# Value pass of an expert layer: one 512-column matmul with both parts of the gated activations in place of two of 256 columns

## The chip, the cores and the metric

The kernel runs on one core of a Trainium2 chip. The metric is the device time of one execution in microseconds (us); the median over several runs counts. The core has five engines that run beside each other and wait for each other on semaphores: TensorE (matmuls, PE in the profile, its weight loads are PEld), VectorE (DVE), ScalarE (ACT), GpSimd (POOL) and SyncE (SP), which issues most of the transfers. Matmul results go to PSUM, which has 8 banks of 512 float32 columns on each of 128 partitions.

## The reference, cut to what matters

Two layers of a decoder trunk over 256 tokens of width 1024. Each has a mixer and then a PEER channel mixer with 128 x 128 = 16384 single-neuron experts. The change lies in the second:

```
def peer(h, w_q, subkeys, u_tab, v_tab):
    ...                                  # top 16 experts for each of 8 heads
    act = gelu(einsum('td,thkd->thk', xc, u_tab[ec]))
    return einsum('thk,thkd->td', gc * act, v_tab[ec])
x = x + peer(h, ...)
```

The kernel gathers nothing. It computes all 16384 activations densely, multiplies them by gates that are zero where an expert was not chosen, and multiplies the result by the whole value table (16384 x 1024).

## The kernel before

**Precision.** The large products are done in a reduced float32 format (fp32r) in which a matmul is one record of the trace; plain fp32 matmuls leave two records each. To keep accuracy each operand is split in a high part (rounded) and a low part (the rest), and three products are summed: high weights by high data, high weights by low data, low weights by high data.

**The stream.** All weights come as tiles of 128 x 1024, 600 in order: `w_in`, `w_out`, `q0`, `u0`, `v0`, `qkv`, `w_o`, `q1`, `u1`, `v1`; `u` and `v` have 128 tiles each. SyncE loads a tile into one of four `raw` buffers as soon as it is free (L346). A tile is handled in halves of 512 columns: ScalarE rounds the high part into `w_hi` (L406), VectorE subtracts to get `w_lo` (L603). There are four half slots, so two tiles are ready or in work at a time. TensorE adds to the semaphore `half_used` at the end of each half, and ScalarE refills on it.

**The value pass** (`combine`, L1168 to L1184, once for each layer, 128 tiles). Tile i of `v` holds the values of 128 experts; their gated activations for 256 tokens are row i of the table `big`. ScalarE rounds a row into `ag_hi` (L537, the first two rows L542), VectorE makes `ag_lo` (L967), both double-buffered and two tiles ahead. TensorE runs over 8 blocks of 128 output channels, m = 0 to 7, and for each over the three products, with 256 token columns: L1180 (`w_hi` by `ag_hi`), L1181 (`w_hi` by `ag_lo`), L1182 (`w_lo` by `ag_hi`). Each matmul has its own load of weights. All three sum into `y_ps[:, m, :]`, 256 columns of PSUM; the eight accumulators lie in banks 0 to 3, two to a bank, and stay there through all 128 tiles. Banks 4 and 5 (`proj_ps`) are for projections, 6 and 7 (`misc_ps`) for the scatter of gates and for sums of squares; they are unused in the value pass.

**Behind the pass.** VectorE waits for the last half, and adds the eight accumulators to the residual `xT` (L980, 8 adds, semaphore `y_added`). ScalarE squares each block of `xT` as it comes (`square`, L436), and TensorE sums the squares with a matrix of ones (`sum_squares`, L1047, plain fp32, 8 matmuls, 16 records, into bank 6). The RMSNorm follows (VectorE L618 to L623, ScalarE L440), then the next projection (`qkv` in layer 0) or the output (layer 1). In layer 0 two tiles of `qkv` are still rounded and split before the adds. GpSimd waits for `y_added` in layer 0 to load the bias rows (L382).

**Before the pass** come the projections of the `u` tiles (L1035 to L1037, the same three products with 256 columns) with the scatter (L1147, plain fp32 matmuls of 60 or 68 columns). The first matmul of the value pass waits for `ag_ready`, which comes only when all gates are applied (`act_gated`, `late_gated`).

Of the kernel before, what the change touches and what calls it, by code (L numbers as in the profile page):

```python
# [21 lines left out]
F32R = mybir.dt.float32r  # L22
I32 = mybir.dt.int32
U32 = mybir.dt.uint32
ALU = mybir.AluOpType
# [3 lines left out]
P = 128  # L29
T = 256  # L30
TT = T // P
D = 1024
KD = D // P
# [41 lines left out]

GROUPS = T // 4


def bucket_of_distance():

    exact, span = REL_BUCKETS // 2, 2048
    out = []
    for n in range(T):
        if n < exact:
            out.append(n)
        else:
            f = np.float32(np.log(np.float32(n) / np.float32(exact))) / np.float32(math.log(span / exact))
            out.append(min(exact + int(np.float32(f * np.float32(REL_BUCKETS - exact))), REL_BUCKETS - 1))
    return out
# [41 lines left out]
def build(nc, a, out):  # L131
    ctx = ExitStack()
    with ctx:
        def sb(name, shape, dt=F32):
            return ctx.enter_context(nc.sbuf_tensor(name, shape, dt))

        def sem(name):
            return ctx.enter_context(nc.semaphore(name))
# [3 lines left out]
        xT = sb("xT", [P, KD, T])  # L142
# [6 lines left out]
        hot_j = sb("hot_j", [P, 8, P])  # L149
        hot_i = sb("hot_i", [P, 8, P])  # L150
        fresh = sb("fresh", [P, 2, T])
        ag_hi = sb("ag_hi", [P, 2, T], F32R)
        ag_lo = sb("ag_lo", [P, 2, T], F32R)
        const = sb("const", [P, 4 * P])
        gains = sb("gains", [P, 5, KD])
        small = sb("small", [P, 6, KC])
# [1 line left out]
        ident, anti, ones, iota = (const[:, P * i:P * (i + 1)] for i in range(4))  # L158

        psum = ctx.enter_context(nc.psum_tensor("psum", [P, 8, 512], F32))  # L160
        y_ps = psum[:, 0:4, :].rearrange("p b (m t) -> p (b m) t", t=T)
        proj_ps = [psum[:, 4 + i, 0:T] for i in range(2)]
        misc_ps = [psum[:, 6 + i, :] for i in range(2)]

# [14 lines left out]
        sq, _ = room(top - 2 * KD * T, KD, T)  # L179
# [69 lines left out]
        sq_ready = [sem(f"sq_ready{i}") for i in range(5)]  # L249
# [42 lines left out]
        hot_step = sem("hot_step")  # L292
        ag_hi_ready = sem("ag_hi_ready")
        ag_ready = sem("ag_ready")
        y_added = sem("y_added")
        staged = sem("staged")
        values_staged = sem("values_staged")
# [101 lines left out]
        def _(act):  # L399
# [29 lines left out]
                        ahead(name, k, j)  # L429
                sweep(act, turns, body)  # L430

            def square(r, sem_, count):

                for m in range(KD):
                    act.wait_ge(sem_, count(m))
                    act.activation(sq[:, m, :], xT[:, m, :], ACT.Square).then_inc(sq_ready[r], 1)  # L436

            def root(r):
                act.wait_ge(rstd_step[r], 2)
                act.activation(rstd[:], ms[:, 1, :], ACT.Sqrt).then_inc(rstd_ready[r], 1)  # L440
# [118 lines left out]
            ids_f_tmp = room(top - 2 * KD * T, UNITS, TOPK)[0]  # L559
            experts(0)  # L560

            square(2, y_added, lambda m: m + 1)
            root(2)
            split_operand(3)
            taking("qkv", lambda k, j: act.activation(z1[:, bass.ds(4 * k + j, 1), :].rearrange("p a t -> p (a t)"), proj_ps[j % 2],
# [23 lines left out]
            split_operand(4)  # L589
            only_ahead("w_o", 2)  # L590
            experts(1)
            square(4, y_added, lambda m: KD + m + 1)
            root(4)


# [1 line left out]
        def _(dve):  # L597
# [287 lines left out]
            def experts(l):  # L885
# [90 lines left out]
                        ahead(v, k, j)  # L976
                sweep(dve, NKEYS // 4, v_body, last=1)
                dve.wait_ge(half_used, 2 * (TILE0[v] + NKEYS))
                for m in range(KD):
                    dve.tensor_tensor(xT[:, m, :], xT[:, m, :], y_ps[:, m, :], ALU.add).then_inc(y_added, 1)  # L980
                dve.wait_ge(y_added, KD * (l + 1))

            add_residual("w_out")
# [37 lines left out]
        def _(pe):  # L1021
# [19 lines left out]
                sweep(pe, tiles // 4, lambda k: [project(name, k, j, operand) for j in range(4)],  # L1041
                      first=0 if operand is None else 1)

            def sum_squares(r):
                for m in range(KD):
                    pe.wait_ge(sq_ready[r], m + 1)
                    mm = pe.matmul(misc_ps[0][:, 0:T], ones, sq[:, m, :], start=(m == 0), stop=(m == KD - 1))  # L1047
                mm.then_inc(ss_ready[r], 1)


# [3 lines left out]
                      start=True, stop=True).then_inc(line_ps, 1)  # L1054
# [13 lines left out]
            for t in range(TT):  # L1068
                for c in range(KC):
                    mm = pe.transpose(psum[:, 2 + t, c * P:(c + 1) * P], vn[:, c, t * P:(t + 1) * P], ident)  # L1070
# [4 lines left out]
            for c in range(KC):  # L1075
                for t in range(TT):
                    for e in range(2):
# [3 lines left out]
                        mm = pe.matmul(o, ones[0:1, 0:HD], sgu_b[0:1, h, :], start=False, stop=True)  # L1081
# [32 lines left out]
            def experts(l):  # L1114
                q, u, v = f"q{l}", f"u{l}", f"v{l}"
                sum_squares(1 + 2 * l)
                pe.wait_ge(subk_in, 16 * (l + 1))

                def q_body(k):
                    for j in range(4):  # L1120
                        project(q, k, j, 2 + 3 * l)
                        if not (isinstance(k, int) and 4 * k + j == 0):
                            score_keys(l, k, j - 1) if j else score_keys(l, k - 1, 3)
                sweep(pe, 4, q_body, first=1)
                score_keys(l, 3, 3)
                projections(u, 4 * PICK_TURNS)
                pe.wait_ge(build_step, 23 * l + 15 + 7)
                for a_, src in enumerate((id_f[:, 0], id_f[:, 1], tv)):
                    for t in range(TT):
                        at = (a_ * TT + t) * P  # L1130
                        mm = pe.transpose(psum[:, at // 512, at % 512:at % 512 + P],
                                          src.rearrange("p (t u) r -> p t (u r)", t=TT)[:, t, :], ident)
                mm.then_inc(picks_ps, 1)

                def scatter(late, g, half):

                    rows = NKEYS - LATE if late else LATE
                    r = 2 * GROUPS * l + (0 if late else GROUPS) + g
                    if late:
                        at_least(pe, gates_stored, GROUPS * l + g - 1)  # L1140
                    elif isinstance(g, int) and g < 2:
                        pe.wait_ge(gates_stored, GROUPS * (l + 1))
                    else:
                        pe.wait_ge(act_gated, GROUPS * l + g - 1)
                    pe.wait_ge(hot_ready, r + 1)
                    for i in range(4):
                        mm = pe.matmul(misc_ps[half][:, i * rows:(i + 1) * rows], hot_j[:, 4 * half + i, :],  # L1147
                                       hot_i[:, 4 * half + i, 0:rows], start=True, stop=True)
                    mm.then_inc(scattered, 1)

                def late_body(k):
                    for j in range(4):
                        project(u, k, j)
                        for half in range(2):
                            scatter(True, 8 * (k - PICK_TURNS) + 2 * j + half, half)

                def early_body(k):
                    for j in range(4):
                        project(u, k, j)
                        if not (isinstance(k, int) and k == LATE_TURN and j == 0):  # L1160
                            scatter(False, 4 * (k - LATE_TURN) + j - 1, (j - 1) % 2)

                sweep_from(pe, PICK_TURNS, LATE_TURN, late_body, first=1)
                sweep_from(pe, LATE_TURN, NKEYS // 4, early_body, first=1)
                for g in range(NKEYS - LATE - 1, GROUPS):
                    scatter(False, g, g % 2)

                def combine(k):  # L1168
                    for j in range(4):
                        n, i = TILE0[v] + 4 * k + j, 4 * k + j  # L1170
                        pe.wait_ge(ag_ready, NKEYS * l + i + 1)
                        begin, end = isinstance(i, int) and i == 0, isinstance(i, int) and i == NKEYS - 1
                        for b in range(2):
                            pe.wait_ge(split_ready, 2 * n + b + 1)
                            s = (2 * j + b) % SPLIT
                            for c in range(4):
                                m = 4 * b + c
                                hi, lo = (w[:, s, c * P:(c + 1) * P] for w in (w_hi, w_lo))

                                pe.matmul(y_ps[:, m, :], hi, ag_hi[:, j % 2, :], start=begin and m % 2 == 0, stop=False, skip_group_check=True)  # L1180
                                pe.matmul(y_ps[:, m, :], hi, ag_lo[:, j % 2, :], start=False, stop=False, skip_group_check=True)  # L1181
                                mm = pe.matmul(y_ps[:, m, :], lo, ag_hi[:, j % 2, :], start=False, stop=end, skip_group_check=True)  # L1182
                            mm.then_inc(half_used, 1)
                sweep(pe, NKEYS // 4, combine, first=1, last=1)  # L1184

            experts(0)
            sum_squares(2)
            projections("qkv", 24, 3)
            pe.wait_ge(proj_taken, PROJ0["w_o"])
            for t in range(TT):  # L1190
                for g in range(2):
                    for i in range(4):
                        mm = pe.transpose(psum[:, 2 * t + g, i * P:(i + 1) * P], z1[:, 16 + 4 * g + i, t * P:(t + 1) * P], ident)
# [35 lines left out]
            pairs(pe, None, scores, outcomes)  # L1229
            projections("w_o", 8, 4)  # L1230
            experts(1)
            sum_squares(4)


# [43 lines left out]
```

## Time and profile before

| | |
|---|---|
| median of 3 runs | 2322.8 us (2320.18 to 2323.11) |
| span of the profiled execution | 2329.5 us |
| its mean granted TensorE clock | 0.965 |
| PE busy | 2168.4 us, 93%, 17092 records |
| PE weight loads busy | 2090.0 us, 90% |
| VectorE busy | 1646.3 us, 71% |
| ScalarE busy | 1037.1 us, 45% |
| HBM traffic | 139 GB/s over the span |

The times of the profile are those of one profiled execution, from the first to the last instruction of the program; it has no separate time beside its span. Busy time is the time in which an engine has an instruction under way; matmuls overlap each other and the loads, so what a matmul costs is read from the distance between starts and not from its duration. The granted clock is a share of 2.4 GHz. The rows on which the prediction rests stand in a section of their own below. In them L12 is line 12 of the kernel, `out<-in` names what an instruction writes and reads, and "idle before" is followed by what ended the idle time.

### The profile page before, as it was taken

How to read it: one execution, taken by the hardware profiler on the slowest of the kernel's cores; microseconds unless marked ns; L12 is line 12 of the kernel's file. 1: busy time of each engine (PE TensorE's matmuls, PEld its weight loads, DVE VectorE, ACT ScalarE, POOL GpSimd, SP SyncE). 2: the span in 40 equal slices, each digit the busy share in tenths (PEclk: the TensorE clock that was granted, in tenths of full speed). 3: DMA queues.
4: the chain of work that ended last, by engine and by line, in shares of the span. 5: the costliest groups of instructions: out<-in, count | busy, mean ns of one | idle time of the engine just before them, and what ended most of it. 6: DMA issues, size and time to landing. Idle time of an engine off the chain costs nothing.

```text
span 2329.5 us, 52851 instructions
## 1 busy us (share of the span) xinstructions
PE 2168.4 (93%) x17092; PEld 2090.0 (90%) x17092; DVE 1646.3 (71%) x3922; ACT 1037.1 (45%) x2162; POOL 19.8 (1%) x43
## 2 busy tenths in 40 slices
PE   6778798999999999999999987989999999999998
PEld 5558788999999999999987677889999999999998
DVE  3657998777888655555544589977788886555555
ACT  4334355444333355555544443544443333555554
POOL 1000000000000000000001000000000000000000
PEclk9779999999999899999998999999999998999999
DMA  5203344333443355555552233433334343555553
GB/s 179 73 23 115 115 162 140 106 107 126 138 141 137 116 180 180 183 185 181 182 184 95 71 111 117 162 128 108 108 128 143 136 143 119 183 184 180 180 182 125
DMA packets 90032, 323.57 MB, mean 139 GB/s; under 512 B 9914, under 2 KB 11994, under 8 KB 89728
## 3 DMA queue, kind: packets, MB, share of 16 engines
q1 hardware_dynamic: 88528, 316.71, 39.8%
q0 software_dynamic: 1456, 6.23, 0.8%
q8 instruction: 29, 0.48, 0.1%
q14 instruction: 19, 0.16, 0.0%
HBM read 321.82 MB, written 1.08 MB: 139 GB/s over the span
## 4 chain that ended last, share of the span: by engine, by line
PE 75%; DVE 12%; issue 9%; ACT 2%; DVEq 1%; DMA 0%; POOL 0%; ACTq 0%; POOLq 0%
PE psum L1180 11%; PE psum L1181 11%; PE psum L1182 11%; PE psum L1035 10%; PE psum L1036 9%; PE psum L1037 9%; PE psum L1147 9%; DVE w_lo L603 2%; DVE big L812 1%; ACT w_hi L406 1%; PE psum L1205 1%; DVE big L824 1%; PE psum L1208 1%; DVE big L819 1%; PE psum L1047 1%
## 5 line engine op out<-in xcount | busy, mean ns | idle before, releaser
L603 DVE TENSOR_TENSOR w_lo<-raw,w_hi 128x512 fp32r<-128x512 f32 x1200 | 781.8, 687 | 245.4 <-ACT w_hi L406 242.5
L1035 PE MATMUL psum<-x_hi,w_hi 128*128 128x256 f32 x2752 | 808.9, 294 | 77.9 <-DVE w_lo L603 44.5
L1036 PE MATMUL psum<-x_lo,w_hi 128*128 128x256 f32 x2752 | 785.3, 285 | 0.0
L1037 PE MATMUL psum<-x_hi,w_lo 128*128 128x256 f32 x2752 | 785.2, 285 | 0.0
L406 ACT ACTIVATE w_hi<-raw 128x512 fp32r<-128x512 f32 x1200 | 685.6, 619 | 39.4 <-PE psum L1037 28.8
L1035 PEld LDWEIGHTS psum<-x_hi,w_hi 128*128 128x128 f32 x2752 | 534.8, 194 | 91.1 <-DVE w_lo L603 57.1
L1180 PE MATMUL psum<-ag_hi,w_hi 128*128 128x256 f32 x2048 | 581.9, 284 | 2.9 <-DVE ag_lo L967 2.9
L1181 PE MATMUL psum<-ag_lo,w_hi 128*128 128x256 f32 x2048 | 581.5, 284 | 0.0
L1182 PE MATMUL psum<-ag_hi,w_lo 128*128 128x256 f32 x2048 | 581.4, 284 | 0.0
L1036 PEld LDWEIGHTS psum<-x_lo,w_hi 128*128 128x128 f32 x2752 | 535.5, 195 | 0.0
L1037 PEld LDWEIGHTS psum<-x_hi,w_lo 128*128 128x128 f32 x2752 | 534.1, 194 | 0.0
L1180 PEld LDWEIGHTS psum<-ag_hi,w_hi 128*128 128x128 f32 x2048 | 395.2, 193 | 3.3 <-DVE ag_lo L967 3.3
L1181 PEld LDWEIGHTS psum<-ag_lo,w_hi 128*128 128x128 f32 x2048 | 395.3, 193 | 0.0
L1182 PEld LDWEIGHTS psum<-ag_hi,w_lo 128*128 128x128 f32 x2048 | 395.3, 193 | 0.0
L967 DVE TENSOR_TENSOR ag_lo<-big,ag_hi 128x256 fp32r<-128x256 f32 x256 | 108.8, 425 | 307.2 <-ACT ag_hi L537 306.3
L1147 PE MATMUL psum<-hot_i,hot_j 128*128 128x68 f32 (+1 forms) x2048 | 262.7, 277 | 12.4 <-DVE big L876 5.4
L1147 PEld LDWEIGHTS psum<-hot_i,hot_j 128*128 128x128 f32 x2048 | 253.7, 197 | 18.8 <-DVE hot_i L870 10.6
L537 ACT ACTIVATE ag_hi<-big 128x256 fp32r (+1 forms) x252 | 105.2, 417 | 366.4 <-PE psum L1182 366.4
L867 DVE TENSOR_TENSOR hot_j<-const,picks 128x512 f32<-128x512 f32 x256 | 174.8, 683 | 0.0
L528 ACT ACTIVATE fresh<-psum 128x256 f32<-128x256 f32 x120 | 46.1, 384 | 279.8 <-PE psum L1037 279.8
L507 ACT ACTIVATE big<-psum 128x256 f32 x136 | 52.1, 383 | 209.7 <-PE psum L1037 209.3
L865 DVE TENSOR_TENSOR hot_i<-const,picks 128x240 f32<-128x240 f32 (+1 forms) x256 | 106.7, 417 | 1.4 <-PE psum L1147 0.7
(149 smaller groups left out, 1156.5 us busy)
## 6 DMA issues: line engine op xcount, KB each, us to landing
raw<-in_peer_u SPq DMA_DIRECT2D x256, 512.0 KB, 3.2
raw<-in_peer_v SPq DMA_DIRECT2D x256, 512.0 KB, 3.4
raw<-in_peer_q SPq DMA_DIRECT2D x32, 512.0 KB, 3.3
raw<-in_w_qkv SPq DMA_DIRECT2D x24, 512.0 KB, 3.2
raw<-in_w_in SPq DMA_DIRECT2D x16, 512.0 KB, 3.5
raw<-in_w_out SPq DMA_DIRECT2D x8, 512.0 KB, 3.3
raw<-in_w_o SPq DMA_DIRECT2D x8, 512.0 KB, 3.3
big<-bias_scratch POOLq DMA_DIRECT2D x1, 3072.0 KB, 12.1
```

The source lines that it names most:

```text
L406: act.activation(w_hi[:, s, :], raw[:, j % RAW, b * HALF:(b + 1) * HALF], ACT.Copy).then_inc(hi_ready, 1)
L603: dve.tensor_tensor(w_lo[:, s, :], raw[:, j % RAW, b * HALF:(b + 1) * HALF], w_hi[:, s, :].bitcast(F32), ALU.subtract).then_inc(split_read ...
L865: dve.tensor_tensor(own_i, numbers[:, :, i0:i0 + rows].to_broadcast([P, 4, rows]), ahead_of[0].to_broadcast([P, 4, rows]), ALU.is_equal).t ...
L867: dve.tensor_tensor(own_j, numbers.to_broadcast([P, 4, P]), ahead_of[1].to_broadcast([P, 4, P]), ALU.is_equal).then_inc(hot_step, 1)
L967: dve.tensor_tensor(ag_lo[:, j % 2, :], big[:, bass.ds(i * T, T)], ag_hi[:, j % 2, :].bitcast(F32), ALU.subtract).then_inc(ag_ready, 1)
L1035: pe.matmul(proj_ps[j % 2], hi, x_hi[:, m, :], start=(m == 0), stop=False)
L1036: pe.matmul(proj_ps[j % 2], hi, x_lo[:, m, :], start=False, stop=False)
L1037: mm = pe.matmul(proj_ps[j % 2], lo, x_hi[:, m, :], start=False, stop=(m == KD - 1))
L1147: mm = pe.matmul(misc_ps[half][:, i * rows:(i + 1) * rows], hot_j[:, 4 * half + i, :], hot_i[:, 4 * half + i, 0:rows], start=True, stop=True)
L1180: pe.matmul(y_ps[:, m, :], hi, ag_hi[:, j % 2, :], start=begin and m % 2 == 0, stop=False, skip_group_check=True)
L1181: pe.matmul(y_ps[:, m, :], hi, ag_lo[:, j % 2, :], start=False, stop=False, skip_group_check=True)
L1182: mm = pe.matmul(y_ps[:, m, :], lo, ag_hi[:, j % 2, :], start=False, stop=end, skip_group_check=True)
```

## The change

In the value pass `ag_hi` and `ag_lo` become the two halves of one buffer `ag_parts`, side by side, so that one matmul of 512 columns multiplies a block of `w_hi` by both. The low product of weights (`w_lo` by `ag_hi`) stays a matmul of 256 columns. So 16 matmuls and 16 weight loads a tile take the place of 24 and 24. Each accumulator is now a whole bank, all eight banks in use: columns 0 to 255 (`y_ps`) hold high by high and low by high, columns 256 to 511 (`y_small_ps`) high by low. Behind the pass VectorE adds both parts to `xT`, 16 adds in place of 8, the large part of one block ahead of the small part of the block before, with a new semaphore `y_large_added`. The blocks are added, squared and summed in the order 6, 7, 0, 1, ..., 5, since bank 6 is also where the sum of squares goes.

```diff
+Y_ORDER = [6, 7, 0, 1, 2, 3, 4, 5]
...
-        ag_hi = sb("ag_hi", [P, 2, T], F32R)
-        ag_lo = sb("ag_lo", [P, 2, T], F32R)
+        ag_parts = sb("ag_parts", [P, 2, 2 * T], F32R)
+        ag_hi, ag_lo = ag_parts[:, :, 0:T], ag_parts[:, :, T:2 * T]
...
-        y_ps = psum[:, 0:4, :].rearrange("p b (m t) -> p (b m) t", t=T)
+        y_ps = psum[:, :, 0:T]
+        y_small_ps = psum[:, :, T:2 * T]
...
-            def square(r, sem_, count):
-
-                for m in range(KD):
-                    act.wait_ge(sem_, count(m))
+            def square(r, sem_, count, order=range(KD)):
+
+                for n, m in enumerate(order):
+                    act.wait_ge(sem_, count(n))
                     act.activation(sq[:, m, :], xT[:, m, :], ACT.Square).then_inc(sq_ready[r], 1)
...
-                for m in range(KD):
-                    dve.tensor_tensor(xT[:, m, :], xT[:, m, :], y_ps[:, m, :], ALU.add).then_inc(y_added, 1)
+                for n in range(KD + 1):
+                    if n < KD:
+                        m = Y_ORDER[n]
+                        dve.tensor_tensor(xT[:, m, :], xT[:, m, :], y_ps[:, m, :], ALU.add).then_inc(y_large_added, 1)
+                    if n > 0:
+                        m = Y_ORDER[n - 1]
+                        dve.wait_ge(y_large_added, KD * l + n)
+                        dve.tensor_tensor(xT[:, m, :], xT[:, m, :], y_small_ps[:, m, :], ALU.add).then_inc(y_added, 1)
...
-                                pe.matmul(y_ps[:, m, :], hi, ag_hi[:, j % 2, :], start=begin and m % 2 == 0, stop=False, skip_group_check=True)
-                                pe.matmul(y_ps[:, m, :], hi, ag_lo[:, j % 2, :], start=False, stop=False, skip_group_check=True)
+                                pe.matmul(psum[:, m, :], hi, ag_parts[:, j % 2, :], start=begin, stop=False, skip_group_check=True)
                                 mm = pe.matmul(y_ps[:, m, :], lo, ag_hi[:, j % 2, :], start=False, stop=end, skip_group_check=True)
```

`sum_squares` takes the same `order`, and both are called with `Y_ORDER` behind the two value passes.

## Rows read from the trace of the kernel before

**Rows 1.** The page: busy time by engine, and the chain by line.

```profile
PE 2168.4 (93%) x17092; PEld 2090.0 (90%) x17092; DVE 1646.3 (71%) x3922; ACT 1037.1 (45%) x2162; POOL 19.8 (1%) x43
...
PE psum L1180 11%; PE psum L1181 11%; PE psum L1182 11%; PE psum L1035 10%; PE psum L1036 9%; PE psum L1037 9%; PE psum L1147 9%; DVE w_lo L603 2%; DVE big L812 1%; ACT w_hi L406 1%; PE psum L1205 1%; DVE big L824 1%; PE psum L1208 1%; DVE big L819 1%; PE psum L1047 1%
```

**Rows 2.** Windows of both value passes: stretch, busy us (records), clock, DMA share, GB/s.

```profile
790.00:796.00 6.00, 6.00 (x29) 6.00 (x30) 0.19 (x1) 0.46 (x2) 0.00 (x0) 0.53 0.00 0
796.00:1161.00 365.00, 365.00 (x3044) 365.00 (x3043) 215.68 (x380) 184.44 (x379) 0.00 (x0) 1.00 0.53 181
...
1945.00:1950.00 5.00, 4.55 (x23) 4.55 (x24) 0.73 (x2) 0.24 (x1) 0.00 (x0) 0.56 0.00 0
1950.00:2316.00 366.00, 366.00 (x3051) 365.84 (x3049) 213.51 (x378) 183.76 (x378) 0.00 (x0) 1.00 0.52 175
```

**Rows 3.** Timeline inside the value pass of layer 0: start us, us, instruction.

```profile
999.87 0.28 PE L1180 MATMUL psum<-ag_hi,w_hi 128*128 128x256 f32 x1
999.88 0.19 PEld L1181 LDWEIGHTS psum<-ag_lo,w_hi 128*128 128x128 f32 x1
999.99 0.28 PE L1181 MATMUL psum<-ag_lo,w_hi 128*128 128x256 f32 x1
...
1000.11 0.28 PE L1182 MATMUL psum<-ag_hi,w_lo 128*128 128x256 f32 x1
...
1000.23 0.28 PE L1180 MATMUL psum<-ag_hi,w_hi 128*128 128x256 f32 x1
```

**Rows 4.** Timeline of its first tiles, TensorE alone, clock 0.5.

```profile
792.00 0.41 PE L1180 MATMUL psum<-ag_hi,w_hi 128*128 128x256 f32 x1
792.21 0.41 PE L1181 MATMUL psum<-ag_lo,w_hi 128*128 128x256 f32 x1
```

**Rows 5.** L1047 behind layer 1: durations min/median/max ns, and its timeline row.

```profile
L1047 PE MATMUL psum<-big,const x16: 379/379/483, 2317.1 to 2320.4; 128*128 128x256 f32 x16
...
2317.09 3.72 PE L1047 MATMUL psum<-big,const 128*128 128x256 f32 x16 [1.04 <-ACT big L436]
```

**Rows 6.** Timeline: loads of 68-column matmuls, then the first projection matmul behind.

```profile
557.04 0.98 PEld L1147 LDWEIGHTS psum<-hot_i,hot_j 128*128 128x128 f32 x8
...
557.95 0.19 PEld L1035 LDWEIGHTS psum<-x_hi,w_hi 128*128 128x128 f32 x1
557.97 0.36 PE L1035 MATMUL psum<-x_hi,w_hi 128*128 128x256 f32 x1
558.06 0.19 PEld L1036 LDWEIGHTS psum<-x_lo,w_hi 128*128 128x128 f32 x1
```

**Rows 7.** Timeline of one tile on ScalarE and VectorE; the page's DMA issue row.

```profile
1000.18 0.42 ACT L537 ACTIVATE ag_hi<-big 128x256 fp32r x1 [1.42 <-PE psum L1182]
...
1000.50 1.14 ACT L406 ACTIVATE w_hi<-raw 128x512 fp32r<-128x512 f32 x2
...
1000.74 0.43 DVE L967 TENSOR_TENSOR ag_lo<-big,ag_hi 128x256 fp32r<-128x256 f32 x1 [1.17 <-ACT ag_hi L537]
...
1001.15 1.29 DVE L603 TENSOR_TENSOR w_lo<-raw,w_hi 128x512 fp32r<-128x512 f32 x2
...
1003.06 0.42 ACT L537 ACTIVATE ag_hi<-big 128x256 fp32r x1 [1.42 <-PE psum L1182]
...
raw<-in_peer_v SPq DMA_DIRECT2D x256, 512.0 KB, 3.4
```

**Rows 8.** Behind the passes: adds and sums in the timeline, and two windows.

```profile
1163.22 2.73 DVE L980 TENSOR_TENSOR xT<-xT,psum 128x256 f32<-128x256 f32 x8
...
1164.14 5.41 PE L1047 MATMUL psum<-big,const 128*128 128x256 f32 x16 [2.83 <-ACT big L436]
...
2316.08 2.73 DVE L980 TENSOR_TENSOR xT<-xT,psum 128x256 f32<-128x256 f32 x8 [3.49 <-PE psum L1182]
...
1163.00:1170.00 7.00, 5.41 (x16) 4.14 (x16) 3.30 (x10) 4.01 (x9) 1.19 (x1) 0.76 0.47 149
...
2316.00:2322.00 6.00, 3.76 (x17) 2.96 (x16) 3.79 (x10) 3.93 (x9) 0.00 (x0) 1.00 0.00 0
```

More of the change, by code:

```diff
@@ L294, in build @@
         ag_ready = sem("ag_ready")
+        y_large_added = sem("y_large_added")
         y_added = sem("y_added")
@@ L560, in _ @@
             experts(0)
-            square(2, y_added, lambda m: m + 1)
+            square(2, y_added, lambda n: n + 1, Y_ORDER)
             root(2)
@@ L591, in _ @@
             experts(1)
-            square(4, y_added, lambda m: KD + m + 1)
+            square(4, y_added, lambda n: KD + n + 1, Y_ORDER)
             root(4)
@@ L1042, in projections, with sum_squares @@
                       first=0 if operand is None else 1)
[L1044 to L1047, printed above, removed]
+            def sum_squares(r, order=range(KD)):
+                for n, m in enumerate(order):
+                    pe.wait_ge(sq_ready[r], n + 1)
+                    mm = pe.matmul(misc_ps[0][:, 0:T], ones, sq[:, m, :], start=(n == 0), stop=(n == KD - 1))
                 mm.then_inc(ss_ready[r], 1)
@@ L1186, in _ @@
             experts(0)
-            sum_squares(2)
+            sum_squares(2, Y_ORDER)
             projections("qkv", 24, 3)
@@ L1231, in _ @@
             experts(1)
-            sum_squares(4)
+            sum_squares(4, Y_ORDER)
 def kernel(x, ev_w_in, ev_conv_w, ev_conv_b, ev_conv_ln_g, ev_conv_ln_b, ev_sgu_ln_g, ev_sgu_ln_b, ev_sgu_w, ev_sgu_b,
```

## The prediction

> **What bounds the kernel now.** I read the page first: the tensor engine is busy 93% of the span, and three matmul lines of the value pass, L1180, L1181 and L1182, each hold 11% of the chain that ended last [rows 1]. A busy share says nothing of what a matmul costs, so the windows table comes next. In the two value passes the tensor engine is busy for the whole stretch, 3044 matmul records in 365.00 us and 3051 in 366.00 us, 0.120 us for one, at a granted clock of 1.00, which is 2.4 GHz [rows 2]. Waits and loop branches that stand between them leave no mark on that mean. So the passes are bound by the pace of the matmuls, and the question is what makes the 0.12 us.
>
> The timeline shows the pattern [rows 3]. A matmul starts, 0.01 us later the load of the next weights starts, and the next matmul starts 0.12 us after the last. A triple (high by high, high by low, low by high) takes 0.36 us, 999.87 to 1000.23. At 2.4 GHz 256 columns, one in a cycle, are 106.7 ns, so 13.3 ns of each 120 are not column time. At a clock of 0.5 (1.2 GHz) the spacing is 0.213 us, which is 256 columns and nothing more [rows 4]. The 13.3 ns are therefore no fixed price of a matmul; they show only where the columns are short.
>
> **What the load costs.** In a train of plain fp32 matmuls of 68 columns eight loads take 0.98 us, so (0.98 - 0.19) / 7 = 0.113 us from load to load: there the load sets the pace, since the columns are much shorter. After that train a load starts at 557.95; its matmul is recorded from 557.97, but lasts 0.36 us where the others last 0.28, so its weights were in place at about 558.05, and at 558.06 the next load starts [rows 6]. A load is thus about 0.10 to 0.11 us, and begins when the matmul before it has taken over its own weights. The nearest row for a long matmul is L1047: plain fp32, each made of two records, 16 of them in 3.72 us. The first lasts 483 ns, the others 379; (3720 - 483) / 15 = 216 ns apart, with one load under each [rows 5]. That is 512 column steps at 2.4 GHz (213.3) and 2.5 ns. A load under a long stream of columns costs nothing there.
>
> **The change, part by part.**
> 1. The main term. Each triple becomes a 512-column matmul and a 256-column one. The columns stay 768; one load and one matmul start go. In the reading I take, 120 ns is the load with its hand-over and hides under the long matmul: that costs 216 ns [rows 5], and the short one behind it still waits until the load that begins at its start is done, for the next long one, 120 ns [rows 3]. 336 in place of 360: 24.2 ns (unrounded, 360 - 215.8 - 120). Of 2048 triples some 16 run at the low clock at the two starts, where the columns bound (27 matmuls to 795.6 us, 22 or so after 1945) and nothing is saved [rows 2, 4]. 2032 x 24.2 ns = 49.2 us. Bounds: 0 if 0.469 ns is the price of a column, and 35 ns a triple (71 us) if the short matmul too fell to 109.
>
> 2. What feeds the passes. A tile falls from 2.88 us (24 x 0.12) to 2.69 us (8 x 0.336). When TensorE ends a tile, ScalarE begins the turn for the tile after the next, at 1000.18 and again at 1003.06. Its work is 0.42 + 1.14 = 1.56 us, VectorE's 0.43 + 1.29 = 1.72 us; the first half of the weights is split at 1001.15 + 0.64 = 1001.80, 1.6 us into the turn, the second at 1002.44, 2.3 us into it [rows 7]. TensorE wants the first of them one tile after the turn began, the second half a tile behind it: at 2.69 and 4.0 us after the change, so 1.1 and 1.7 us are to spare. Both engines' work stays under 2.69 us. A load lands 3.4 us after its issue, with four tiles (10.8 us) in flight. Cost 0; if that cover failed, a tile would still take no more than what is longest of these, the 2.3 us turn, and that is under 2.69.
>
> 3. The accumulators. Each of the eight gets a bank, four of which the projections and the scatter used. The first matmul of the pass waits already for the gated activations, and these for the last reads of those banks. No wait is added: 0.
>
> 4. The adds. Eight adds of 256 columns become sixteen. Eight start to end are 2.73 us, (2.73 - 0.41) / 7 = 0.33 us each [rows 8]. Their result is wanted a tile at a time by ScalarE's squares and by L1047, so not all of it is path. In layer 1 adds begin at 2316.08 and L1047 ends at 2317.09 + 3.72 = 2320.81, 4.73 us. After the change the last small add starts 15 x 0.33 = 4.97 us in; from there, as with the first add now, 1.1 us to its sum (the square, the load) and 0.6 for two records: 6.7 us, +2.0. In layer 0 the sum ends 6.3 us after the first add now, since the mean clock is 0.76 there [rows 8]; adds pace it as well then: +0.5 with the same clock. Together +2.5 us. Nothing excludes the low clock for all of L1047, as its matmuls now come with gaps: 8 x 0.853 us (each sum 4 x 0.213 [rows 4]) behind a first sum that is 0.66 us later, 8.9 us, +4.2 and +2.6, so +6.8 is the upper bound; the lower is +2.0 (layer 0 free). Each small add waits on a semaphore for the large add before last, done by then. Behind the adds on VectorE stands only the norm, on POOL the load of the bias rows, which no one reads before the 24 `qkv` tiles are through.
>
> 5. The order of the sum (bank 6 and 7 first) puts L1047's own bank among the first to be read; it moves no work. The one buffer for both parts changes addresses only: 0.
>
> Sum: -49.2 + 2.5 = -46.7 us. The profiled execution spans 2329.5 us, 6.7 above the median of 2322.8; from it the sum gives 2282.8, and from the median, to which I put it, 2276.1 us.
>
> **The rivals.**
> A, forecast: the load hides, 336 ns a triple, 2276.
> B, half the gain: load and columns disturb each other. The columns here are read one in a cycle of 2.4 GHz, in the plain rows at half that rate, so L1047 [rows 5] can't exclude that a load costs the stream 13.3 ns, and 106.7 + 13.3 is just 120. A load still stands under each matmul: 226.7 + 120 = 346.7 ns. 2032 x 13.3 = 27.1 us; 2322.8 - 27.1 + 2.5 = 2298.2. For it: the round number, and that a load under a plain stream was quicker (0.11) than here. Against it: 0.11 us of load behind a start that is 0.01 us late comes to 0.12 without any disturbance.
> The Trainium skill, TensorE: Matmul & The Clock Gate, section Part 2: What happens when you issue a matmul, says that TensorE has separate read ports for weights and columns, so a load takes nothing from a running matmul. By that rule B falls and the sum is A's; the trace agrees for plain fp32 (216 ns), and no row shows it for this type.
> C, no change: 0.469 ns is what a column costs in this type (120 / 256). 512 cost 240, the triple stays 360, and only the adds count: 2325.3. The low clock would hide that too [rows 4]. Against it: nothing needs it, since a load accounts for the 120.
> D, slower: C, and the sparse sums of squares after the passes run at the low clock (part 4, +6.8): 2329.6. It decides once the passes give back under 3.3 ns a triple (6.8 / 2032 us); for it is the 0.76 of layer 0, against it the 1.00 of layer 1 [rows 8].
> E, more: the load for the next long matmul is ready earlier, and the short one costs 109, as its columns do: 325 a triple, 71.1 us, 2254.2. Against it: no load [rows 3] begins before the matmul ahead of it.
> The same section's subsection Back-to-back issue gap gives N/2.4 + 2.5 ns for a matmul in a stream at full clock, 216 and 109 ns, which is E's triple; the trace agrees at 512 steps and not at 256, where it has 120.
>
> **How the numbers follow.** A 0.47, B 0.35, C 0.09, D 0.06, E 0.03. Predicted 2276. A with its adds is 2275.6 to 2280.4, B 2297.7 to 2302.5; some room below for a short matmul between 109 and 120 (3.3 ns a triple are 7 us). 2269 to 2303 holds A and B, 0.82, and leaves out C, D and E. Under 0.2% (4.6 us) this kernel's runs can't be told apart: faster 0.85 (A, B, E), same 0.09 (C), slower 0.06 (D).
>
> **What would show it.** After: the long matmul's starts 216 ns ahead of the short one's (227 is B, 240 is C), the short one's 120 ahead of the next; 16 matmuls a tile and 2.69 us; windows of the passes at clock 1.00 with VectorE and ScalarE idle between turns as now; a value pass of about 347 us where it is 371; sixteen adds at 0.33 us and L1047 ending 2 us later behind them. A tensor engine idle before the first half of a tile would break part 2, a clock under 1.00 inside a pass the main term.

## The result, and the profile after

| | before | changed |
|---|---|---|
| median of 20 runs | 2323.22 us (2318.14 to 2331.25) | 2309.99 us (2297.06 to 2326.07) |
| ratio | | 0.9938, 95% interval 0.9920 to 0.9955 |
| span of the profiled execution | 2329.5 us | 2303.9 us |

The change makes the kernel 13 us, 0.6%, faster, the way that was forecast. The forecast was 47 us, with 2269 to 2303 as its range; the median lies 7 us above the range. Single executions of the changed kernel fall in groups: two at 2297 and 2298, six from 2303.9 to 2305.6, nine from 2309.6 to 2311.1, and three above. Before, the groups are at 2318.5, 2323 and 2331.

The windows over the two value passes of the changed kernel (stretch, busy us and records of PE, PEld, DVE, ACT and POOL, clock, DMA share, GB/s) answer to [rows 2]:

```profile
796.00:1148.00 352.00, 352.00 (x2033) 307.86 (x2032) 215.99 (x380) 185.09 (x380) 0.00 (x0) 1.00 0.57 188
1930.00:2288.00 358.00, 358.00 (x2029) 310.44 (x2027) 213.72 (x378) 183.79 (x378) 0.00 (x0) 1.00 0.54 179
```

TensorE has still no idle time and the clock is 1.00, so nothing starves the pass. But about the same number of matmuls takes 352 us in layer 0 and 358 in layer 1. The timeline of layer 0 (start, us, instruction) answers to [rows 3]:

```profile
1000.23 0.39 PE L1190 MATMUL psum<-ag_parts,w_hi 128*128 128x512 f32 x1
1000.46 0.27 PE L1191 MATMUL psum<-ag_parts,w_lo 128*128 128x256 f32 x1
1000.57 0.40 PE L1190 MATMUL psum<-ag_parts,w_hi 128*128 128x512 f32 x1
1000.80 0.28 PE L1191 MATMUL psum<-ag_parts,w_lo 128*128 128x256 f32 x1
1000.92 0.39 PE L1190 MATMUL psum<-ag_parts,w_hi 128*128 128x512 f32 x1
```

Long to short is 0.23 us, short to long 0.11 to 0.12. In layer 1 every third cycle is slower, 0.36 us from long to long (2000.03 to 2000.39 and 2001.09 to 2001.45), the others 0.35:

```profile
2000.03 0.40 PE L1190 MATMUL psum<-ag_parts,w_hi 128*128 128x512 f32 x1
2000.27 0.28 PE L1191 MATMUL psum<-ag_parts,w_lo 128*128 128x256 f32 x1
2000.39 0.40 PE L1190 MATMUL psum<-ag_parts,w_hi 128*128 128x512 f32 x1
2000.63 0.28 PE L1191 MATMUL psum<-ag_parts,w_lo 128*128 128x256 f32 x1
2000.74 0.40 PE L1190 MATMUL psum<-ag_parts,w_hi 128*128 128x512 f32 x1
...
2001.09 0.40 PE L1190 MATMUL psum<-ag_parts,w_hi 128*128 128x512 f32 x1
...
2001.45 0.40 PE L1190 MATMUL psum<-ag_parts,w_hi 128*128 128x512 f32 x1
```

From here on I use windows of 300 us inside each pass, TensorE alone (busy us and records, clock, DMA share, GB/s). The count holds two or three matmuls that reach in from outside. Of the kernel before:

```profile
820.00:1120.00 300.00, 300.00 (x2503) 1.00 0.53 182
1960.00:2260.00 300.00, 300.00 (x2503) 1.00 0.55 182
```

and of the changed kernel:

```profile
820.00:1120.00 300.00, 300.00 (x1733) 1.00 0.58 189
1960.00:2260.00 300.00, 300.00 (x1700) 1.00 0.56 186
```

300 us / 2500 is 120.0 ns before. After, 300 / 1731 is 173.3 ns a matmul, 346.7 a triple, in layer 0, and 300 / 1698 is 176.7 ns, 353.3 a triple, in layer 1. In every stretch of each pass the mean stays the same to 0.1 ns: a pass picks one value and keeps it.

The adds behind the pass, changed kernel, layer 1, answer to [rows 8]:

```profile
2288.55 0.75 DVE L986 TENSOR_TENSOR xT<-xT,psum 128x256 f32<-128x256 f32 x2 [3.38 <-PE psum L1191]
...
2290.22 5.02 PE L1057 MATMUL psum<-big,const 128*128 128x256 f32 x16 [1.71 <-ACT big L440]
```

From the first add to the end of the sum of squares it is 6.69 us, where it was 4.73: +1.96. In layer 0 it is 7.54 where it was 6.33: +1.2.

The two profiled spans differ by 25.6 us, twice the difference of the medians. The passes, first start to last end, give 371.4 - 357.0 = 14.4 and 370.6 - 363.7 = 6.9 us; from the end of the first pass to the start of the second it is 784.1 us before and 776.4 after, 7.8 less. (The first pass begins 1.5 us later after, and what follows the last pass is 2.0 us longer, which makes up the 25.6.) Between the passes the program is the same apart from the adds. The execution before had its clock down for 17 us in the attention, from 1253 on, and the one after had not. The window of 1235 to 1275, all five engines, before and after:

```profile
1235.00:1275.00 40.00, 37.48 (x181) 25.87 (x179) 14.67 (x30) 15.19 (x38) 4.39 (x11) 0.79 0.24 80
1235.00:1275.00 40.00, 36.42 (x165) 21.34 (x166) 20.69 (x48) 17.16 (x56) 8.68 (x20) 1.00 0.08 27
```

In the kernel of experiment 5, which keeps the matmuls of before and changes where they accumulate and how they are added, that stretch between the passes is 776.5 us too. So the 7.8 us belong to where the clock fell in the one execution and not to the change.

### The profile page after: what moved, and what is told of

Its sections match the earlier page's. It is cut to its first block, busy times and chain, and to the rows that moved or that the text cites. A ratio compares the mean times of both kernels' runs of the same rounds, so it can differ in the third digit from the quotient of the medians.

```text
span 2303.9 us, 48771 instructions
## 1 busy us (share of the span) xinstructions
PE 2139.5 (93%) x15044; PEld 1969.8 (85%) x15044; DVE 1652.5 (72%) x3938; ACT 1038.8 (45%) x2162; POOL 19.8 (1%) x43
## 4 chain that ended last, share of the span: by engine, by line
PE 75%; DVE 13%; issue 9%; ACT 2%; DVEq 1%; DMA 0%; POOL 0%; ACTq 0%; POOLq 0%
PE psum L1190 21%; PE psum L1191 10%; PE psum L1045 10%; PE psum L1046 10%; PE psum L1047 10%; PE psum L1157 8%; DVE w_lo L607 2%; DVE big L816 1%; ACT w_hi L410 1%; DVE big L828 1%; PE psum L1214 1%; DVE big L823 1%; PE psum L1057 1%; DVE big L729 1%; PE psum L1217 1%
## 5 line engine op out<-in xcount | busy, mean ns | idle before, releaser
L1047 PE MATMUL psum<-x_hi,w_lo 128*128 128x256 f32 x2752 | 784.8, 285 | 0.0
L1190 PE MATMUL psum<-ag_parts,w_hi 128*128 128x512 f32 x2048 | 720.4, 398 | 2.9 <-DVE ag_parts L971 2.9
L1191 PE MATMUL psum<-ag_parts,w_lo 128*128 128x256 f32 x2048 | 572.6, 280 | 0.0
L1047 PEld LDWEIGHTS psum<-x_hi,w_lo 128*128 128x128 f32 x2752 | 533.9, 194 | 0.0
L1190 PEld LDWEIGHTS psum<-ag_parts,w_hi 128*128 128x128 f32 x2048 | 386.1, 189 | 96.3 <-DVE ag_parts L971 3.3
L1191 PEld LDWEIGHTS psum<-ag_parts,w_lo 128*128 128x128 f32 x2048 | 387.4, 189 | 0.0
L971 DVE TENSOR_TENSOR ag_parts<-big,ag_parts 128x256 fp32r<-128x256 f32 x256 | 108.7, 425 | 285.7 <-ACT ag_parts L541 284.8
L541 ACT ACTIVATE ag_parts<-big 128x256 fp32r (+1 forms) x252 | 105.2, 418 | 344.9 <-PE psum L1191 344.9
L871 DVE TENSOR_TENSOR hot_j<-const,picks 128x512 f32<-128x512 f32 x256 | 175.4, 685 | 0.0
L874 DVE TENSOR_TENSOR hot_i<-hot_i,picks 128x240 f32<-128x240 f32 (+1 forms) x256 | 107.0, 418 | 0.0
```

The lines of the kernel that those rows point to most:

```text
L871: dve.tensor_tensor(own_j, numbers.to_broadcast([P, 4, P]), ahead_of[1].to_broadcast([P, 4, P]), ALU.is_equal).then_inc(hot_step, 1)
L874: dve.tensor_tensor(own_i, own_i, ahead_of[2].to_broadcast([P, 4, rows]), ALU.mult).then_inc(hot_ready, 1)
L971: dve.tensor_tensor(ag_lo[:, j % 2, :], big[:, bass.ds(i * T, T)], ag_hi[:, j % 2, :].bitcast(F32), ALU.subtract).then_inc(ag_ready, 1)
L1047: mm = pe.matmul(proj_ps[j % 2], lo, x_hi[:, m, :], start=False, stop=(m == KD - 1))
L1190: pe.matmul(psum[:, m, :], hi, ag_parts[:, j % 2, :], start=begin, stop=False, skip_group_check=True)
```

## The experiments

All edits are to the changed kernel, and the code is cut to the lines that matter. "A pass" is from its first matmul's start to its last one's end.

**1. The same kernel again.** No edit.

> The changed kernel once more, nothing edited. Its first trace has a triple (one long and one short matmul) at 346.7 ns through the whole of layer 0's value pass and at 353.3 ns through the whole of layer 1's. Theory 'load': a weight load under a stream of 2.4 GHz costs the stream 13.3 ns, 346.7 is the rule and 353.3 a disturbed pass of that one execution; then a second trace shows 346.7 in at least one pass, and whichever pass has more is chance. Theory 'layer': something in layer 1 (addresses, what runs beside) makes it 353.3; then layer 0 is again 346.7 and layer 1 again 353.3, and times of single executions don't scatter by more than those of before.

```profile
820.00:1120.00 300.00, 300.00 (x1732) 1.00 0.57 189
1960.00:2260.00 300.00, 300.00 (x1733) 1.00 0.57 189
```

Both passes are 357.0 us, 346.7 ns a triple, and the span is 2294.9 us. Five executions gave 2296.6 to 2311.1 (ratio to before 0.9934, 0.9908 to 0.9960). So it is not the layer: the same program has 346.7 or 353.3 in layer 1, with nothing here that decides it. One pass at 353.3 costs 1016 x 6.7 ns = 6.8 us, and the groups of single times of the changed kernel, 2297, 2305 and 2311, lie 6 to 8 us apart, as none, one and two such passes would. The kernel before has groups too, though all its matmuls are 120.0 ns apart, and there the mean clock goes with the group (about 0.970 near 2318.5, 0.967 near 2323, 0.965 near 2331). In the changed kernel it does not: it is 0.967 and 0.968 in the two fastest executions and 0.967 to 0.970 in the nine near 2310. That speaks for the passes as the cause, but no trace of an execution with two slow passes was taken, so it is inferred.

**2. Long matmuls only.**

```diff
-mm = pe.matmul(y_ps[:, m, :], lo, ag_hi[:, j % 2, :], ...)
+mm = pe.matmul(psum[:, m, :], lo, ag_parts[:, j % 2, :], ...)
```

> Both products of a block use 512 columns (low weights by both parts too, which adds the low by low product and more TensorE work): 16 matmuls a tile, all long, each with one load. Theory 'hidden' (the forecast): a load under a long stream costs nothing, 216 ns each, a pass of 2048 x 0.216 = 442 us. Theory 'load': 213.3 + 13.3 = 226.7 ns each, 464 us. Theory 'column': a column costs 0.4514 (346.7/768) to 0.469 ns (120/256), 231 to 240 ns each, 473 to 492 us.

A window of each pass:

```profile
820.00:1120.00 300.00, 300.00 (x1326) 1.00 0.43 144
2100.00:2400.00 300.00, 300.00 (x1325) 1.00 0.44 145
```

300 / 1323.5 = 226.7 ns, in both layers, and both passes are 466.3 us. One execution was timed, 2517.4 us, with more columns than the changed kernel has. The forecast's 216 is wrong; "load" has it exactly.

**3. 384 columns twice.** The first matmul of each accumulator keeps 512.

```diff
-pe.matmul(psum[:, m, :], hi, ag_parts[:, j % 2, :], ...)
-mm = pe.matmul(y_ps[:, m, :], lo, ag_hi[:, j % 2, :], ...)
+pe.matmul(psum[:, m, 0:384], hi, ag_parts[:, j % 2, 0:384], ...)
+mm = pe.matmul(psum[:, m, 0:384], lo, ag_parts[:, j % 2, 0:384], ...)
```

> Both products of a block use 384 columns (half of the low part of the activations is left out, low weights by half of the low part is added). 16 matmuls a tile. 'Hidden': 160 + 2.5 = 162.5 ns each, a pass of 333 us. 'Load': 160 + 13.3 = 173.3 ns each, 355 us. 'Column' at 0.469: 180 ns, 369 us; at 0.4514 it is 173.3 as well, so this run tells the two apart only together with the 512-column one: from 384 to 512 columns 'load' adds 53.3 ns, 'column' 57.8 to 60.

```profile
820.00:1120.00 300.00, 300.00 (x1733) 1.00 0.57 189
1960.00:2260.00 300.00, 300.00 (x1733) 1.00 0.57 189
```

173.3 ns in both passes, which are 357.4 us; one execution was timed, 2297.5 us. With 120.0 at 256 columns and 226.7 at 512, each step of 128 columns adds 53.3 ns, which is 128 cycles of 2.4 GHz, and 13.3 ns are left over at every length. "Column" falls. What is left is a price for each matmul with its load; since every matmul of runs 2 and 3 has one load of 128 weights, they can't tell a price of the load from one of the matmul itself. Run 6 bears on that.

**4. Four long, then four short.**

```diff
 for c in range(4):
-    pe.matmul(psum[:, m, :], hi, ag_parts ...); pe.matmul(y_ps[:, m, :], lo, ag_hi ...)
+    pe.matmul(psum[:, m, :], hi, ag_parts ...)
+for c in range(4):
+    pe.matmul(y_ps[:, m, :], lo, ag_hi ...)
```

> The changed kernel with the four long matmuls of a half first and its four short ones behind them; same work, same loads. 'Load': the price hangs on the loads alone, so long to long 226.7 ns, short to short 120, and the pass stays at 347 us (ratio to the changed kernel 1.00). 'Column': 231 to 240 and 115.6 to 120. If instead a load is slow only under a stream that is no longer than itself, long to long is 216, short to short 120, and the pass is 344 us.

```profile
820.00:1120.00 300.00, 300.00 (x1713) 1.00 0.56 187
1960.00:2260.00 300.00, 300.00 (x1712) 1.00 0.56 187
```

Passes of 361.2 and 360.8 us, 300 / 1710 = 175.4 ns a matmul in both, 350.8 a triple. In the trace long to long has a mean of 233.7 and short to short 118.7. So none of the numbers expected came out: "load" is right for trains of one length through a whole pass, and in a mixed one more comes on top, here 4.2 ns a triple. The single times are close together, 2305.2 to 2306.5, ratio to before 0.9927 (0.9898 to 0.9956).

**5. The accumulators and the adds alone.**

```diff
-pe.matmul(psum[:, m, :], hi, ag_parts[:, j % 2, :], ...)
+pe.matmul(y_ps[:, m, :], hi, ag_hi[:, j % 2, :], ...)
+pe.matmul(y_small_ps[:, m, :], hi, ag_lo[:, j % 2, :], ...)
```

> Only the new place of the accumulators (all eight banks, high and low part apart), the order of the blocks and the sixteen adds; the value pass keeps its three 256-column matmuls with three loads. All theories on the long matmul: matmuls stay 120.0 ns apart (whatever the bank), both passes 371 us, and only the adds cost: +2 to +3 us, 0.1% slower than before. If the gain of the change were in the banks (two accumulators of one bank no longer share it), the spacing would fall below 120.

```profile
820.00:1120.00 300.00, 300.00 (x2503) 1.00 0.54 182
1960.00:2260.00 300.00, 300.00 (x2502) 1.00 0.54 182
```

120.0 ns apart, passes of 370.6 and 370.5 us: the banks give nothing. The ratio is 1.0012 (1.0000 to 1.0024), +2.8 us with an interval of 0 to 5.6, which agrees with part 4 of the forecast and can't fix its size.

**6. Half the weight columns.** The three products of before, with 64 of 128 weight columns. Half of the output is left out; eight matmuls of full size begin each pass and are not shown.

```diff
+h = P // 2
-pe.matmul(psum[:, m, :], hi, ag_parts[:, j % 2, :], ...)
-mm = pe.matmul(y_ps[:, m, :], lo, ag_hi[:, j % 2, :], ...)
+pe.matmul(psum[0:h, m, 0:T], hi[:, 0:h], ag_hi[:, j % 2, :], ...)
+pe.matmul(psum[0:h, m, 0:T], hi[:, 0:h], ag_lo[:, j % 2, :], ...)
+mm = pe.matmul(psum[0:h, m, 0:T], lo[:, 0:h], ag_hi[:, j % 2, :], ...)
```

> The three 256-column matmuls of before, each with only the first 64 of its 128 weight columns (half the output channels are left out; the stream is as long as before). The load is half as long. 'The load takes its reads from the stream' (price by the weight): 106.7 + 6.7 = 113.3 ns apart, a pass of 350 us. 'Hand-over' (a fixed price for each change of weights): 120, 371 us. 'The load itself is the limit' (my forecast's reading of the 120): the stream's 109, 337 us.

```profile
820.00:1120.00 300.00, 300.00 (x2574) 1.00 0.56 187
1960.00:2260.00 300.00, 300.00 (x2649) 1.00 0.57 192
```

113.3 ns in layer 1, 6.7 over the columns: half the weights, half the price. In layer 0 it is 116.7, 10.0 over the columns. It is neither the stream's 109 nor a fixed 120 (passes 362.3 and 352.1 us, one execution timed, 2307.1 us). So the price is not one for each matmul whatever it loads, which speaks for a load that takes turns from the stream. It is not shown beyond that: with half the weights half the results are written as well, and no run keeps one of the two while it changes the other, or runs an fp32r matmul without a load. And here a pass has one of two values too, with all its matmuls of one length.

**7. Long, long, short, short.**

```diff
-long(c), short(c) for c in 0, 1, 2, 3
+long(0), long(1), short(0), short(1), long(2), long(3), short(2), short(3)
```

> The changed kernel with its matmuls in the order long, long, short, short. Trains of equal length kept 226.7 and 173.3 and 120 to the tenth, alternating ones 346.7 or 353.3 a triple by pass, four and four 350.8. Theory 'each change of length may cost a step of 6.7 ns': with half as many changes of length as the alternating order it lies between 346.7 and 351 and scatters less, 357 to 361 us a pass. Theory 'phase at the clock switch': 346.7 or 353.3 in any order, by chance of the pass.

```profile
820.00:1120.00 300.00, 300.00 (x1725) 1.00 0.58 188
1960.00:2260.00 300.00, 300.00 (x1725) 1.00 0.58 188
```

300 / 1722.5 = 174.2 ns in both layers, 348.3 a triple, passes of 358.7 and 358.3 us. That is between 346.7 and 351 as the first theory has it. The single times run from 2301.9 to 2311.6 (ratio 0.9940, 0.9918 to 0.9962), so the kernel as a whole doesn't scatter less. But the scatter need not be in the passes: the profiled execution (2310.5 us, mean clock 0.963) had its clock down for 17 us in the attention, and from pass to pass it is 785.6 us where run 1 has 776.3. The four others near 2310 have mean clocks of 0.962 to 0.965, the one at 2301.9 has 0.967. Whether their passes differ, one trace can't tell.

**8. No low clock at the start of a pass.**

```diff
+fill(5)                        # plain matmuls into an unused bank
 for g in range(NKEYS - LATE - 1, GROUPS):
     scatter(False, g, g % 2)
+    fill(2)
+fill(1)
```

> The changed kernel with 16 idle plain matmuls (ones by constants into an unused bank) put in where TensorE waits during the last gates ahead of each value pass, 5 before the last five scatters, 2 behind each, 1 at the end. Their result is not used. If they hold the clock at 1.00 until the pass begins, the first 16 triples no longer run at 0.213 us a 256 columns: a pass begins about 1 us earlier and is 2.8 us shorter, together 5 to 8 us for both layers. Theory 'phase at the clock switch': with no switch inside a pass all passes and executions show the same spacing, 346.7 or 353.3, and single times scatter less. Otherwise the mix of 346.7 and 353.3 stays.

The changed kernel's TensorE ahead of the first pass and at its start, first two lines, then this kernel's, with both passes:

```profile
778.00:788.00 10.00, 6.75 (x35) 0.68 0.21 76
788.00:795.00 7.00, 5.56 (x21) 0.50 0.01 2
```

```profile
778.00:788.00 10.00, 9.88 (x64) 1.00 0.15 52
788.00:795.00 7.00, 7.00 (x40) 1.00 0.07 15
...
820.00:1120.00 300.00, 300.00 (x1700) 1.00 0.55 185
1960.00:2260.00 300.00, 300.00 (x1733) 1.00 0.56 189
```

The clock stays at 1.00 from ahead of the pass on. A pass at 353.3 is 362.1 us (363.7), one at 346.7 is 355.3 (357.0), and the first begins at 787.9 us (789.3 to 791.4). Seven executions: 2297.6 to 2315.3, median 2304.1, ratio 0.9926 (0.9904 to 0.9949). The saving is 1.7 us a pass, less than the 2.8 expected, and the ratio can't be told from the changed kernel's. With no switch of the clock inside a pass, layer 0 has 353.3 and layer 1 346.7: the switch is not what picks the value. The profiled execution is the one at 2297.6, with one slow pass and a mean clock of 0.975. Five of the other six are at 2304.0 to 2305.3 with 0.975 or 0.976, one step of 6.8 us above it, where two slow passes would put them.

**9 and 10. Turned round: activations as weights, value tiles as the stream.** 10 adds the filling matmuls of 8.

```diff
-hi, lo = (w[:, s, c * P:(c + 1) * P] for w in (w_hi, w_lo))        # c in range(4)
-pe.matmul(psum[:, m, :], hi, ag_parts[:, j % 2, :], ...)
-mm = pe.matmul(y_ps[:, m, :], lo, ag_hi[:, j % 2, :], ...)
+hi, lo = (x[:, j % 2, t * P:(t + 1) * P] for x in (ag_hi, ag_lo))  # t in range(2)
+pe.matmul(psum[:, 2 * t + b, :], hi, w_hi[:, s, :], ...)
+pe.matmul(psum[:, 2 * t + b, :], lo, w_hi[:, s, :], ...)
+mm = pe.matmul(psum[:, 2 * t + b, :], hi, w_lo[:, s, :], ...)
...
+pe.transpose(psum[:, Y_BANK[m], t * P:(t + 1) * P], y_sb[:, 2 * t + b, c * P:(c + 1) * P], ident)  # 16
```

> The value pass turned round: the gated activations (128 experts by 128 tokens, four of them a tile: high and low, two token blocks) are the weights, and halves of the value tile (512 channels, high and low) stream past them. 12 matmuls a tile, all of 512 columns, 12 loads. The sums then have tokens on the partitions, so behind the pass four copies and sixteen transposes come ahead of eight adds. Rule 'columns at 2.4 GHz and 13.3 ns for a load': 12 x 226.7 = 2.720 us a tile where the changed kernel has 8 x 346.7 = 2.773 or 8 x 353.3 = 2.827; a pass of 348.2 us and 2.7 for the cold start, 351 (357.0 and 363.7). And since all matmuls are alike, all passes of all executions show the same spacing. The turning costs 4 to 6 us a pass, so the kernel is 0 to 20 us faster than the changed one: 2292 to 2305. 'Column' at 0.4514: 231.1 ns each, 358 us a pass. If each matmul's spacing also varies by pass here, equal lengths are not what locks it.

> The same with the 16 filling matmuls ahead of each pass. They took the pass of the changed kernel from 357.0 to 355.3 us (and 363.7 to 362.1) and let it begin 1.5 to 3.5 us earlier, so 5 to 8 us less than the turned kernel without them, and passes of 349 us with no low clock in them.

Windows of 9:

```profile
820.00:1120.00 300.00, 300.00 (x1325) 1.00 0.58 192
1960.00:2260.00 300.00, 300.00 (x1326) 1.00 0.58 193
```

and of 10, first pass:

```profile
820.00:1120.00 300.00, 300.00 (x1325) 1.00 0.58 193
```

226.7 ns in all four passes of the two kernels. Passes are 350.2 and 349.8 us in 9, and 348.45 in both layers in 10 (348.2 by the rule). Behind the pass of layer 1, kernel 9:

```profile
2277.61 1.29 DVE L988 COPY big<-psum 128x512 f32<-128x512 f32 x2 [3.17 <-PE psum L1192]
...
2278.35 1.97 PE L1199 MATMUL psum<-const,big 128*128 128x128 f32 x16 [0.78 <-DVE big L988]
2278.83 2.74 DVE L991 TENSOR_TENSOR xT<-xT,psum 128x256 f32<-128x256 f32 x8
...
2280.16 3.62 PE L1058 MATMUL psum<-big,const 128*128 128x256 f32 x16
```

From the first copy to the sum's end it is 6.2 us, less than the sixteen adds of the changed kernel (6.7), since copies, transposes and adds overlap; the expectation had 4 to 6 us on top. The times: 9 has 2295.4 us (2294.2 to 2296.0, ratio 0.9895, 0.9878 to 0.9911), 10 has 2288.7 us (2288.1 to 2289.8, ratio 0.9866, 0.9850 to 0.9883), 6.7 us less, within the 5 to 8 expected. Both are faster than the kernel before and the changed one: their intervals lie below its 0.9920 to 0.9955. Their four executions each scatter by under 2 us, where twenty of the changed kernel scatter by 29 us and the five of run 1 by 14.5. Both traces have a low clock in the attention, as run 7's has, for 20.5 us; from pass to pass they take 787.3 and 786.2 us, against 776.3 in run 1. So their times hold some 10 us that the profiled executions of the changed kernel do not have. Whether chance or the edit puts the low clock there, no run shows.

**11. Short ahead of long.**

```diff
-pe.matmul(psum[:, m, :], hi, ag_parts[:, j % 2, :], start=begin, ...)
-mm = pe.matmul(y_ps[:, m, :], lo, ag_hi[:, j % 2, :], start=False, ...)
+pe.matmul(y_ps[:, m, :], lo, ag_hi[:, j % 2, :], start=begin, ...)
+mm = pe.matmul(psum[:, m, :], hi, ag_parts[:, j % 2, :], start=False, ...)
```

> The changed kernel with the short matmul of a block ahead of its long one. The cycle long, short, long, short is the same but for its beginning. If 346.7 or 353.3 is decided by how the pass begins in time and not by the program, both turn up again, by pass and by execution (2297, 2304, 2311 us). If the beginning long matmul is what leaves the phase to chance, all passes show one value. 'Load' has no other value for either.

Both passes of the trace are at 346.7. The four times are 2296.8, 2297.4, 2303.1 and 2304.2: two pairs, 6.5 us apart at mean clocks of 0.968 and 0.969, so some passes were at 353.3 by all appearance. Which matmul begins doesn't settle it either. Ratio 0.9920 (0.9902 to 0.9939).

## Why the prediction was wrong

**Part 1, the main term, is the step that failed**: "In the reading I take, 120 ns is the load with its hand-over and hides under the long matmul: that costs 216 ns." It costs 226.7 (run 2). The 13.3 ns are not the end of a load that outlasts a short stream; they come on top of the columns, at 256, 384 and 512 alike (runs 2 and 3), and fall to 6.7 and 10.0 ns in the two passes with half the weights (run 6). So a triple saves the 13.3 ns of one matmul with its load and not 24.2, and the term is 27 us in place of 49. This was rival B, at 0.35, with its 346.7 to the tenth.

The row that misled was L1047's 216 ns [rows 5]. Its matmuls are plain fp32, in which 256 columns take those 216 ns; here the columns alone come to 106.7. The prediction names that difference under B and still lets the row decide. The second thing held against B was that 0.11 us of load and 0.01 us of delay make 0.12. That was a near coincidence of two prices; 106.7 + 13.3 = 120.0 was the exact one, and it held to the tenth over 3000 matmuls [rows 2]. The prediction sets beside it a rule of the Trainium skill (TensorE: Matmul & The Clock Gate, section Part 2: What happens when you issue a matmul): weights and columns have separate read ports, so the load takes no read bandwidth from the running matmul. It read this as "a load costs the matmul no time", and that doesn't hold here for the fp32r stream at 2.4 GHz: 226.7 ns measured against 213.3 of columns. Whether the time is lost in the reads or behind them, no run shows.

**What no case had**: a mixed train has more than one pace. Of the eight profiled passes with long and short in turn (the changed kernel twice, runs 8 and 11), six were at 346.7 and two at 353.3. No rival had two values for one program. Each one at 353.3 gives back a quarter of B's gain, 6.8 us of 27. B's own time, with the adds as measured (1.96 + 1.2 = 3.2), is 2323.2 - 27.1 + 3.2 = 2299.3; with one slow pass 2306.1, with two 2312.9. The median of 2310.0 lies between the last two, and the fastest group, 2297 to 2298, is near B. Run 5, which has the adds and all else but the long matmul, gives 2324.9 - 27.1 = 2297.8, with one slow pass 2304.6, with two 2311.4: the three groups. So some 22 us of the miss are shown in the traces (27 and not 49 us); the other 11 or so, from B to the median, rest on the steps between the groups. The range ended at 2303 because it took B as one number.

**Part 2 (what feeds the pass)** was right: idle time before the long matmuls is 2.9 us in 2048, as before, at a tile of 2.77 to 2.83 us.

**Part 3 (the accumulators)** was right: no wait came, and the banks change nothing (run 5).

**Part 4 (the adds)** was right: +2.0 forecast and +1.96 measured in layer 1, +0.5 and +1.2 in layer 0, and +2.8 us (0 to 5.6) for the kernel in run 5 against +2.5.

**Part 5** was right as far as run 5 shows it. **Rivals C and D** fall with runs 2 and 3. **Rival E**: the short matmul's slot was indeed under 120, 0.11 to 0.12, but the long one's was as much longer, so the triple had B's sum. The formula that the prediction sets beside E, N/2.4 + 2.5 ns, is the Trainium skill's for matmuls back to back, but the subsection that it names (TensorE: Matmul & The Clock Gate, Back-to-back issue gap) calls it the gap of an isolated matmul and sets it apart from a stream of loads and matmuls. Here no fp32r matmul in a stream came to it (120.0, 173.3 and 226.7 ns against 109, 162.5 and 216).

**Open** remains what makes a pass take 346.7 or 353.3, or with half the weights 113.3 or 116.7. It is not the layer (run 1), not a clock switch in the pass (run 8), and, by the single times, not which matmul begins (run 11). Steps of 6.7 and 3.3 ns are 16 and 8 cycles of 2.4 GHz, and within a pass the time from long to long repeats in the trace: 343 and 350 ns in turn in layer 0 of the changed kernel, 361, 349 and 350 in its layer 1. A relative phase of load and stream, set as the pass begins, would fit; no run shows it. Passes with full loads and one length of matmul (runs 2, 3, 5, 9, 10 and the kernel before) showed one pace each time.

## What to carry to other kernels

Count the matmuls, each with its load of 128 weights, in full-rate fp32r streams and charge each 13.3 ns over the columns, at 256 to 512 of them; merging two 256-column matmuls on the same weights saves that once, and not the whole gap between 120 ns and the long stream's share. Choose as weights the operand that needs fewer loads and leaves all matmuls at 512 columns: 12 equal ones a tile did in 2.72 us what 8 long and 8 short did in 2.77 to 2.83, and in four executions each the two kernels that do so scattered by under 2 us. When the row that prices a term differs from the new instruction in a respect that a rival names, that row can't decide against the rival.

## What the runs showed of the hardware

An fp32r matmul with its load of 128 weights takes, in a stream at 2.4 GHz, 13.3 ns more than its columns (120.0, 173.3 and 226.7 ns for 256, 384 and 512 columns), and at 1.2 GHz nothing more [rows 4]. Passes in which long and short matmuls alternate keep a pace of 346.7 or 353.3 ns a pair for all of their 1000 pairs; two executions of one program differ in it, and it moves this kernel by 7 us a pass. In the attention the clock falls for 17 to 20.5 us in five of the thirteen traces (the kernel before, runs 6, 7, 9 and 10) and not in the others, which is worth 8 to 9 us between the passes (784.1 and 785.6 us before and in run 7, 776.3 in run 1).
